# mLSTM values stored beside a column of ones: state and normaliser as one product, sample denominators from queries times n

## The reference

```
s     = (q k^T) * exp(d_log - m_t)
num   = w_inter * (q C) + s v
den   = w_inter * (q . n) + sum_j s_ij
h     = num / max(|den|, exp(-m_t))
C_new = decay * C + sum_c w_k k_c v_c^T
n_new = decay * n + sum_c w_k k_c
```

## Time and profile before

| what | value |
|---|---|
| median of three runs | 4469.44 us |
| the profiled execution | 4459.9 us, of which span 4458.2 us |
| mLSTM stage | about 1006 to 1290 us |
| PE busy over the span | 4313.8 us |
| ScalarE busy | 1276.9 us |
| POOL busy | 959.8 us |
| mean granted TensorE clock | 0.965 of full |

### The profile page before, as it was taken

The page is one execution under the profiler, slowest core; times in us unless marked ns, Lnnn a source line. Parts: engine busy times, 40 slices in busy tenths (PEclk is TensorE's granted clock), DMA queues, the critical chain, the costliest instruction groups (busy, mean ns, idle before and its releaser), DMA issues.

```text
span 4458.2 us, 70608 instructions
## 1 busy us (share of the span) xinstructions
PE 4313.8 (97%) x29748; PEld 3989.2 (89%) x29748; DVE 2859.9 (64%) x3898; ACT 1276.9 (29%) x1431; POOL 959.8 (22%) x619
## 2 busy tenths in 40 slices
PE   6999999999989699999999999999999999999997
PEld 3777777776679699999999999999999999999997
DVE  2488212313453522888888588887787788888885
ACT  2000101211122112333444444443333333333332
POOL 1000000001100000000000222226777455545420
PEclk8999999997779899999999999999999999999998
DMA  9111211117752222566666588889999999989983
GB/s 385 45 57 57 81 50 62 57 57 256 281 209 101 73 76 85 184 207 203 202 206 206 196 318 326 320 308 374 389 379 391 328 334 327 334 323 330 331 320 146
DMA packets 248785, 993.99 MB, mean 223 GB/s; under 512 B 42921, under 2 KB 127337, under 8 KB 168729
## 3 DMA queue, kind: packets, MB, share of 16 engines
q1 hardware_dynamic: 152376, 652.83, 41.1%
q0 software_dynamic: 48320, 279.88, 16.4%
q10 hardware_dynamic: 47904, 58.74, 3.6%
HBM read 917.71 MB, written 73.64 MB: 222 GB/s over the span
## 4 chain that ended last, share of the span: by engine, by line
PE 92%; DMA 4%; DVE 3%; issue 1%; POOL 1%; ACT 0%; SPq 0%; DVEq 0%; ACTq 0%; POOLq 0%
PE PS L2258 13%; PE PS L2259 13%; PE PS L2260 13%; PE PS L2128 12%; PE PS L2347 6%; PE PS L2349 6%; PE PS L2348 6%; PE PS L2131 5%; PE PS L1892 2%; PE PS L2237 2%; PE PS L2239 2%; PE PS L2238 2%; PE PS L2321 1%; DMA arena<-in_w_ada 1%; PE PS L2212 1%; PE PS L2168 1%
## 5 line engine op out<-in xcount | busy, mean ns | idle before, releaser
L2258 PE MATMUL PS<-h_hi,blk_hi 128*128 128x256 f32 (+1 forms) x4608 | 1376.3, 299 | 41.7 <-DVE h_lo L1633 32.3
L2259 PE MATMUL PS<-h_lo,blk_hi 128*128 128x256 f32 (+1 forms) x4608 | 1366.5, 297 | 0.0
L2260 PE MATMUL PS<-h_hi,blk_lo 128*128 128x256 f32 (+1 forms) x4608 | 1366.2, 296 | 0.0
L2258 PEld LDWEIGHTS PS<-h_hi,blk_hi 128*128 128x128 f32 x4608 | 876.8, 190 | 44.9 <-issue 22.1
L2259 PEld LDWEIGHTS PS<-h_lo,blk_hi 128*128 128x128 f32 x4608 | 877.4, 190 | 0.0
L2260 PEld LDWEIGHTS PS<-h_hi,blk_lo 128*128 128x128 f32 x4608 | 876.7, 190 | 0.0
L1639 DVE TENSOR_TENSOR blk_lo<-arena,blk_hi 128x2048 fp32r<-128x2048 f32 x272 | 623.3, 2292 | 265.2 <-ACT blk_hi L1022 263.7
L744 POOL DMA_INDIRECT arena<-in_peer_v,attw x256 | 475.5, 1858 | 829.5 <-DVE arena L1755 750.9
L2347 PE MATMUL PS<-co_hi,ev_hi 128*128 128x320 f32 x2048 | 634.6, 310 | 7.1 <-DVE ev_lo L1789 6.6
L2348 PE MATMUL PS<-co_lo,ev_hi 128*128 128x320 f32 x2048 | 634.0, 310 | 0.0
L2349 PE MATMUL PS<-co_hi,ev_lo 128*128 128x320 f32 x2048 | 634.0, 310 | 0.0
(11 more groups left out here) (438 smaller groups left out, 4751.1 us busy)
## 6 DMA issues: line engine op xcount, KB each, us to landing
arena<-in_peer_ut SPq DMA_DIRECT2D x256, 1024.0 KB, 5.3
arena<-in_peer_v SPq DMA_DIRECT2D x256, 512.0 KB, 7.1
arena<-in_w_ada SPq DMA_DIRECT2D x48, 2048.0 KB, 9.3
arena<-in_w_f SPq DMA_DIRECT2D x17, 2048.0 KB, 8.2
activation_scratch<-arena ACTq DMA_DIRECT2D x128, 160.0 KB, 7.5
gate_scratch<-arena ACTq DMA_DIRECT2D x10, 2048.0 KB, 14.0
arena<-activation_scratch SPq DMA_DIRECT2D x32, 640.0 KB, 8.9
arena<-gate_scratch SPq DMA_DIRECT2D x32, 640.0 KB, 11.7
```

Source lines behind the costliest of these rows:

```text
L2258: mm(out, hi[:, c], h_part[0][:, c, cols], start=c == 0, stop=False)
L2259: mm(out, hi[:, c], h_part[1][:, c, cols], start=False, stop=False)
L2260: ins = mm(out, lo[:, c], h_part[0][:, c, cols], start=False, stop=c == KC - 1)
```

## The change

- The mLSTM values are stored as `mv1`, [128, 5 tiles, 6 heads, 129], whose last column of each head is one. ScalarE writes the ones once, and its copies of the value tiles go to two strips of 128 columns.
- State and normaliser products become one product of 129 columns, for the prompt (L2182, L2183) and for the samples (L2212, L2213).
- For the samples' denominators, POOL multiplies the weighted queries by n (128x64, n broadcast over the 8 tokens of a sequence) into `m_qn`, and PE sums over partitions by one product with `ones`. This replaces the 8 products with `m_nbs`, which is gone with the copy that made it. The multiplication waits for `ml_kw`, and stands ahead of the masking of the keys.
- `ml_spread` is now raised behind the copy of n into the state tile. The arena behind the values moves by 32 columns.

```diff
-        SM = MV + NT * 768
+        SM = MV + NT * HEADS * (P + 1) + 2
...
+        mv1 = at(MV, NT * HEADS * (P + 1)).rearrange("p (n h c) -> p n h c", h=HEADS, c=P + 1)
...
-                pool.tensor_copy(cs[:, :, P], m_nin[:, h])
-                pool.tensor_copy(m_nbs, m_nin[:, h].unsqueeze(2).broadcast_to([P, NSEQ, P])).then_inc(ml_spread, 1)
+                pool.tensor_copy(cs[:, :, P], m_nin[:, h]).then_inc(ml_spread, 1)
                 pool.wait_ge(ml_kw, h + 1)
+                pool.tensor_tensor(seqs(m_qn), seqs(m_qw[:, TP:T]), m_nin[:, h].unsqueeze(2).broadcast_to([P, NSEQ, SLEN]),
+                                   ALU.mult)
...
+                    if n >= 3:
+                        out, product = mv1[0:nr, j, h:h + 2, 0:P], product.rearrange("p (h c) -> p h c", c=P)
+                    act.activation(out, product, ACT.Copy).then_inc(z_out, 1)
...
+                        act.activation(mv1[:, :, :, P], ones[:, 0:NT * HEADS].rearrange("p (n h) -> p n h", h=HEADS), ACT.Copy)
...
-                    mm(bank(b_, lo, P), m_kw[:, n], mvT[:, n, v], start=True, stop=True)
-                    ins = mm(bank(b_, lo + P, 1), m_kw[:, n], ones[:, 0:1], start=True, stop=True)
+                    ins = mm(bank(b_, lo, P + 1), m_kw[:, n], mv1[:, n, h], start=True, stop=True)
...
-                for pair, vv, st in ((0, mvT[0:TS, 4, v], lambda b: m_Cs[:, h % 2, b, 0:P]),
-                                     (1, ones[0:TS, :], lambda b: m_nbs[:, b])):
-                    out = tail(pair)
-                    mm(out, vv, m_D[0:TS, TP:T], start=True, stop=True)
-                    for b in range(NSEQ):
-                        ins = mm(out[:, SLEN * b:SLEN * b + SLEN], st(b), m_qw[:, TP + SLEN * b:TP + SLEN * b + SLEN],
-                                 start=False, stop=True, skip_group_check=True)
+                out = tail(0)
+                mm(out, mv1[0:TS, 4, h, 0:P], m_D[0:TS, TP:T], start=True, stop=True)
+                for b in range(NSEQ):
+                    mm(out[:, SLEN * b:SLEN * b + SLEN], m_Cs[:, h % 2, b, 0:P], m_qw[:, TP + SLEN * b:TP + SLEN * b + SLEN],
+                       start=False, stop=True, skip_group_check=True)
+                mm(tail(1), ones[0:TS, :], m_D[0:TS, TP:T], start=True, stop=False)
+                ins = mm(tail(1), ones[:, :], m_qn, start=False, stop=True)
...
-                    mm(bank(b_, lo, P), m_kwm[:, b], mvT[0:TS, 4, v], start=True, stop=True)
-                    ins = mm(bank(b_, lo + P, 1), m_kwm[:, b], ones[0:TS, 0:1], start=True, stop=True)
+                    ins = mm(bank(b_, lo, P + 1), m_kwm[:, b], mv1[0:TS, 4, h], start=True, stop=True)
```

More of the change, by code:

```diff
@@ L134, in build @@
         sq = at(GV, 2 * T).rearrange("p (b t) -> p b t", t=T)
-        gvT, mvT = (at(x, NT * 768).rearrange("p (n c) -> p n c", c=768) for x in (GV, MV))
+        gvT = at(GV, NT * 768).rearrange("p (n c) -> p n c", c=768)
+        mv1 = at(MV, NT * HEADS * (P + 1)).rearrange("p (n h c) -> p n h c", h=HEADS, c=P + 1)
         wsmall = at(GV + 2 * T, KC * 70).rearrange("p (c n) -> p c n", n=70)
@@ L167, in build @@
         m_nb = at(r2 + 516 + 2064, 3 * P).rearrange("p (n c) -> p n c", c=P)
-        m_nbs = at(r2 + 516 + 2064 + 384, NSEQ * P).rearrange("p (n c) -> p n c", c=P)
+        m_qn = at(r2 + 516 + 2064 + 384, TS)
         m_kwm = at(r2 + 516 + 2064 + 384 + 1024, NSEQ * P, TS).rearrange("p (n c) -> p n c", c=P)
@@ L897, in job_out @@
                     nr = P if j < 4 else TS
-                    lo = WT * (n % 3)
-                    act.activation((gvT if n < 3 else mvT)[0:nr, j, lo:lo + WT], bank(job % 2, 0, WT, nr),
-                                   ACT.Copy).then_inc(z_out, 1)
+                    lo, h = WT * (n % 3), 2 * (n % 3)
+                    out, product = gvT[0:nr, j, lo:lo + WT], bank(job % 2, 0, WT, nr)
+                    if n >= 3:
+                        out, product = mv1[0:nr, j, h:h + 2, 0:P], product.rearrange("p (h c) -> p h c", c=P)
+                    act.activation(out, product, ACT.Copy).then_inc(z_out, 1)
             for u in range(len(TILES)):
@@ L2163, in _ @@
                 q_, k_ = zF[:, Z_MQ + h], zF[:, Z_MK + h]
-                v = slice(P * h, P * h + P)
                 for pair, r in ((0, 3), (1, 4), (2, 2)):
@@ L2193, in _ @@
                     lo = P * n
-                    for pair, vv, st in ((0, mvT[:, n, v], lambda n: m_C2[h % 2][:, n, 0:P]), (1, ones[:, :], lambda n: m_nb[:, n])):
+                    for pair, vv, st in ((0, mv1[:, n, h, 0:P], lambda n: m_C2[h % 2][:, n, 0:P]), (1, ones[:, :], lambda n: m_nb[:, n])):
                         out = bank(2 * pair, lo, P)
```

## The result

The changed kernel takes 4437.14 us, median of four runs (4434.85 to 4439.17), against 4470.75 us for the kernel before with its four runs. The ratio is 0.9929 with a 95% interval of 0.9914 to 0.9944, so 32 us less (25 to 38). Forecast was 4439. In a later session the ratio was 0.9941 (0.9926 to 0.9956), 26 us less.

The account below looks back on a forecast made before the run. The prediction took PE to bound the kernel, with DVE and loads close behind at certain points. Terms of 2.8, 11.4 and 12.4 made 26.6 us, with the clock 30.0: 4469.4 to 4439, range 4424 to 4455.

Parts of the forecast that it names:

- three signs named as showing the forecast wrong: 129-column pairs at 0.3 us or more at full clock, w_ada waits over 8 us, or stage mean clock below 0.68.
- Prompt states: Four one-column pairs a head go between ada tile products; gain limited by room to the next load, 2.8 us.
- Rival 2: In the mLSTM stage the loads bind, landing more slowly as heads shorten; gain 20 us, time 4449, chance 0.17.
- Denominators: Samples' denominators shrink to two 64-column pairs: 1.66 us a head, 3.1 in head 0, 11.4 us in all.
- Sample states: Eight pairs a head go behind `ml_o`, 3.4 us at 1.2 GHz, limited by DVE in heads 2 to 5; 12.4 us.
- Clock: Sample states (step 7) reach full clock in about the two heads where that counts; 3.4 us, bounds 0 and 12.
- rival 1: Clock rises further, through the ada tiles behind the sample states; gain 38.6 us, time 4431, chance 0.15.
- Rival 3: Odd pitch makes 129-column pairs twice as dear, so terms for prompt and sample states vanish; time 4458, chance 0.07.
- Rival 4: Small products are nearly free, weight loads hidden behind neighbours; gain 6 us, time 4463, chance 0.03.
- rival 5: Slower: new waits keep the stage's clock at 1.2 GHz for longer; 41 us slower, time 4510, chance 0.05.

Follow-up runs that it names:

- half loads: Changed kernel loading only the first half of each w_ada tile in the mLSTM stage, so gates and shifts differ; ratio to the kernel before 0.9920.
- layout alone: Changed kernel with all three product edits undone, only the values' layout left; ratio to the kernel before 0.9991.
- reordered kernel: Changed kernel, head 2's DVE reading moved behind the reciprocal, heads 3 to 5's fourth ada tile behind the sample states; ratio to the kernel before 0.9930.

## Why the prediction was right

The time came out at 4437 for 4439, and the main steps hold: removed pairs of few columns had the price of full ones, DVE and the loads took back part of the gain at the places named, and the clock rose for the states. That the sum came so close is in part luck. Terms that were too small and too large cancel, 2.8 us of the stage's gain lies ahead of the first edited product, and one of the three signs named as showing the forecast wrong did appear. With the earlier trace rows as basis, by terms:

1. **Prompt states, 2.8 us.** Undoing them adds 1.2 us of stage, none of it behind the lead, and no time that the uncertainty lets see. Right in kind: the room to the next load is the price, not the pairs. But waits for w_ada came to 10.1 us (8.2 in the second profile), above the 8 that I had named as showing me wrong. The step that failed is that outside term 1's place the loads stay as far apart as before. The second ada tile behind the states of heads 0 and 1 ran at full clock, 1.93 us for 3.64 (rows below). So PE came sooner to tiles 6, 7 and 12 and had to wait for them; for tile 12 it was 2.19 us. Rival 2 was right in part: with half loads the time is some 9 us shorter, with about 10 of uncertainty.
2. **Denominators, 11.4 us.** The new pair costs 0.36, not 0.22, so 1.5 us a head and 9 in all for the pairs at full clock. Doing them alone gives 15 us in time and 15 to 19 in stage; undoing them costs 16.0 us of stage and some 8 in time. What goes beyond 9 fits the clock, which undoing them brought to half for the states of all six heads. I had booked it to term 4 without saying that this edit brings it.
3. **Sample states, 12.4 us.** The places where DVE takes over were right (5.3 us at tile 16, forecast 5; 2.7 and 2.0 at the broadcasts, forecast about 1). The size is not settled: undoing them, once the denominators are changed, moves the stage by 0 in two profiles and the time by 11 us, with 7 of uncertainty. I had priced the pairs at the low clock, where they are 0.43 a pair, while the denominators' edit brings 0.22 where the clock is up. And head 5's broadcasts, 3.51 us before, fell to half the clock behind the new wait, 6.66 us, which no term had. The wait isn't needed for that: with the sample states undone they took 6.66 us in one profile, too, with no wait ahead.
4. **Clock, 3.4 us.** I had the two heads where it counts, 0 and 1, at full clock; head 0's states were, head 1's were not (2.0 and 3.7 us). Head 0 gave 14.3 us where my terms had 6.5. Of these 7.8 us 2.8 are the lead, and 1.7 are the second ada tile behind the states (rival 1 in part; the first tile stayed at 3.49 us). Head 5 lost 1.1 where they had 3.1 of gain, 4.2 less; heads 1 and 2, with the new waits for w_ada, gave 3.4 less. So these differences cancel, and the stage gave 27.0 where I had summed 30.0.

The second ada tile behind the states of head 1, before and after:

```profile
1107.04 3.64 PE L1892 MATMUL PS<-arena,silu 128*32 128x256 f32 x32
```

```profile
1093.34 1.93 PE L1897 MATMUL PS<-arena,silu 128*32 128x256 f32 x32
```

By heads, my terms without the clock give 6.5, 5.9, 2.1, 4.8, 4.4 and 3.1 us; the profiles 14.3, 4.3, 0.3, 4.4, 4.8 and -1.1. POOL's new product took 0.29 us (forecast 0.3), and the masking was never awaited. Rival 3 is out: layout alone costs no time that the runs show, and a pair of 129 columns took 0.25 us. Rival 4 is out: without the four one-column pairs the prompt states take 0.81 us less. The clock of the stage did not fall, 0.77 (0.75 in the second profile) for 0.72, so rival 5 is out too.

Rows of clock answer to the earlier trace rows (length, busy per engine, clock, DMA share, GB/s), in the changed kernel at the states of heads 0 and 1:

```profile
1042.00:1045.00 3.00, 3.00 (x24) 2.72 (x24) 2.04 (x5) 0.00 (x0) 0.00 (x0) 1.00 0.92 382
1083.00:1086.00 3.00, 3.00 (x14) 2.77 (x14) 1.93 (x5) 0.00 (x0) 0.00 (x0) 0.50 0.92 388
```

The same instructions follow the same ones in both, at 2.4 and at 1.2 GHz. The Trainium skill (TensorE: Matmul & The Clock Gate, section "HAM oscillation — how this bites in real kernels") ties a fall of the clock to idle gaps of PE; these rows show none, with 3.00 of 3.00 us busy in both. With one pass of eight 8-column pairs left in each head, the clock holds in some heads and executions and falls in others (states of head 3: 2.0 in one profile of the changed kernel, 3.7 in the other).

Open: why the runs of the kernel with the sample states undone are some 11 us above the changed kernel's while two profiles show equal stages; how much of the half-load gain is clock; and why the clock of head 0's lead differs between executions.

## What to carry to other kernels

In this kernel a float32 product with one or eight columns cost about as much as one with 128 (0.20 to 0.24 against 0.22 us at full clock). So a column of ones beside the values was nearly free, 0.03 us a pair, and one product with ones over queries times n was cheaper than eight thin ones. Follow each saving to the next load or other engine's signal: PE was busy for 44 us less, and the stage became 27 us shorter. When products are removed or moved, look at the granted clock of the dense work behind them: behind thin products it was at half here. Check with dense fillers whether that clock is on the path at all. And compare the profiled execution's time with the median before a stage of one profile is set against a time.

## What the runs showed of the hardware that was not expected

- With eight more pairs of 8 columns ahead, the following dense products ran at half the clock for all or most of their length in 6 of 6 heads (3.1 to 3.7 us for 2.0); with eight more pairs of 128 columns at the same pace they ran at full in 6 of 6.
- Broadcasts behind one ada tile (heads 4 and 5) ran at half the clock in both profiles of the changed kernel (6.40 to 6.66 us), and once before too; behind two (heads 1 to 3, and in the reordered kernel heads 4 and 5 as well) they took 3.45 to 3.75. One tile ahead isn't enough for the fall, though: head 5 before took 3.51, and head 4 with the denominators undone 3.46.
- The same PE instructions at the start of head 0 took 12.94 to 15.81 us in different executions, with PE busy and no edit ahead of them.
- A load of 2 MB took 12.3 us from issue to landing in the changed kernel, when its neighbour was issued 3 us before it; the slowest before was 11.4.
